# Moving the compressed keys and values of one attention stage ahead of its first scores, on one Trainium2 core

## The reference

```python
kc = einsum('bnlgd,lde->bnge', k_cmp[:, gidx] + cmp_pe[:, None, :], cmp_wk)   # 15 windows of 32 tokens, stride 16
vc = einsum('bnlgd,lde->bnge', v_cmp[:, gidx] + cmp_pe[:, None, :], cmp_wv)
s = q @ kc * scale + bias ; p_cmp = masked_softmax(s) ; o_cmp = p_cmp @ vc      # compressed
o_sel, o_win = ...            # selected blocks and window: with 256 tokens both are dense and causal
o = sum([o_cmp, o_sel, o_win] * sigmoid(h @ w_gate))                           # three gates per head
```

## Time and profile before

| | us |
|---|---|
| three runs | 1266.78, 1266.91, 1272.68 |
| median | 1266.91 |
| the profiled execution's own time | 1268.52 |
| its span in the trace | 1266.7 |
| mean granted TensorE clock | 0.965 |

### The profile page before, as it was taken

The page is one execution under the profiler, slowest core; times in us unless marked ns, Lnnn a source line. Parts: engine busy times, 40 slices in busy tenths (PEclk is TensorE's granted clock), DMA queues, the critical chain, the costliest instruction groups (busy, mean ns, idle before and its releaser), DMA issues.

```text
span 1266.7 us, 19978 instructions
## 1 busy us (share of the span) xinstructions
PE 1159.9 (92%) x8358; PEld 1049.2 (83%) x8358; DVE 933.0 (74%) x1630; ACT 589.4 (47%) x968; POOL 74.4 (6%) x106
## 2 busy tenths in 40 slices
PE   2798798999998977899999989999989988999996
PEld 1687468999897975699999979999979967999996
DVE  5967868888786955598888688887765957765445
ACT  1534655434355455554445464454452365444443
POOL 0000000000000000079000000000000000000000
PEclk8799899999999989999999999999999998999998
DMA  9982335788882960357889637779732452665730
GB/s 375 364 358 74 152 128 196 299 319 286 310 331 100 374 225 1 136 203 277 315 202 368 245 139 296 293 273 292 279 140 101 105 177 85 254 233 200 194 133 34
DMA packets 40810, 280.83 MB, mean 222 GB/s; under 512 B 4736, under 2 KB 5264, under 8 KB 7952
## 3 DMA queue, kind: packets, MB, share of 16 engines
q1 hardware_dynamic: 37296, 269.27, 58.5%
q0 software_dynamic: 2416, 7.92, 2.2%
q10 hardware_dynamic: 1008, 2.37, 0.5%
HBM read 277.91 MB, written 1.10 MB: 220 GB/s over the span
## 4 chain that ended last, share of the span: by engine, by line
PE 69%; DVE 19%; ACT 6%; DMA 5%; issue 1%; SPq 0%; DVEq 0%; ACTq 0%
PE PS L408 68%; DVE LO L1352 5%; DMA raw<-WS 4%; DVE raw L1342 4%; ACT HI L940 2%; DMA SC<-scratch 1%; DVE TMP L1417 1%; DVE SC L1556 1%; DVE TMP L1452 1%; DVE HLo L1412 1%; ACT HH L940 1%; ACT SQ L940 1%; ACT SC L940 1%; DVE SC L1541 1%; DVE RS L1556 1%
## 5 line engine op out<-in xcount | busy, mean ns | idle before, releaser
L408 PE MATMUL PS<-HH,HI 128*128 128x256 f32 x1748 | 502.0, 287 | 25.6 <-ACT HH L940 22.3
L408 PE MATMUL PS<-HLo,HI 128*128 128x256 f32 x1748 | 503.3, 288 | 0.9 <-DVE HLo L1412 0.3
L408 PE MATMUL PS<-HH,LO 128*128 128x256 f32 x1748 | 499.3, 286 | 0.0
L1352 DVE TENSOR_TENSOR LO<-raw,HI 128x1024 fp32r<-128x1024 f32 x340 | 403.8, 1226 | 116.1 <-ACT HI L940 115.9
L940 ACT ACTIVATE HI<-raw 128x1024 fp32r<-128x1024 f32 x340 | 339.8, 1048 | 93.8 <-PE PS L408 64.8
L408 PEld LDWEIGHTS PS<-HH,HI 128*128 128x128 f32 x1748 | 340.0, 195 | 34.9 <-DVE LO L1352 18.9
L408 PEld LDWEIGHTS PS<-HLo,HI 128*128 128x128 f32 x1748 | 339.3, 194 | 4.2 <-DVE HLo L1412 2.9
L408 PEld LDWEIGHTS PS<-HH,LO 128*128 128x128 f32 x1748 | 339.8, 194 | 3.4 <-issue 0.5
L1342 DVE CUSTOM_DVE_ANT_0 raw<-raw,CB,SM 128x1024 f32<-128x1024 f32 x168 | 210.5, 1285 | 24.5 <-DMA raw<-WS 24.5
L408 PE MATMUL PS<-HI,HDH 128*128 128x512 f32 x352 | 140.4, 399 | 0.0
L408 PE MATMUL PS<-HI,HDL 128*128 128x512 f32 x352 | 139.6, 397 | 0.0
(11 more groups left out here) (230 smaller groups left out, 1023.1 us busy)
## 6 DMA issues: line engine op xcount, KB each, us to landing
raw<-WS SPq DMA_DIRECT2D x255, 1024.0 KB, 5.5
SC<-scratch POOLq DMA_DIRECT2D x2, 1024.0 KB, 13.4
FB<-gates_out POOLq DMA_DIRECT2D x3, 512.0 KB, 5.1
SQ<-gates_out POOLq DMA_DIRECT2D x3, 512.0 KB, 9.4
X<-xT ACTq DMA_DIRECT2D x1, 1024.0 KB, 6.9
SC<-ssm POOLq DMA_DIRECT2D x2, 512.0 KB, 5.0
out<-TMP SPq DMA_DIRECT2D x2, 512.0 KB, 2.6
CB<-vecs SPq DMA_DIRECT2D x1, 512.0 KB, 6.5
```

What stands on the lines that cost most here:

```text
L408: return e.matmul(o, l, r, start=start, stop=stop, skip_group_check=True)
L1352: e.tensor_tensor(LO[:, s % HL, :], raw_half(j, h), HI[:, s % HL, :].bitcast(fp32), O.subtract).then_inc(*D.up(("lo", s)))
```

## The change

TensorE: `cmp_keys` and `cmp_values` become `cmp_inputs`, called once ahead of step 0. It does 32 products in turns: key product j into partitions 0 to 63 and value product j into partitions 64 to 127 of one bank, each with 64 columns of weights and 30 moving columns, and signals `cmp_used` with the last. The values so come out turned, with the head's width on the partitions; a new `cmp_spread` in step 0 moves one key head to the upper partitions and transposes the values. The gate products and their two transposes become `gate_values` in step 1, behind the scores of pair 1. ScalarE: three copies out of the bank in `cmp_inputs` ahead of step 0, `cmp_spread` (two copies) after the exponentials of unit 0, the gates' exponential after those of unit 1. VectorE: the windows are formed after ab 3 and ab 4; after ab 7 it says `done` for the chunk at once and calls `low(walk.spare(8))`, ahead of `gate("f0", ...)` and of step 0; the gates' sum and reciprocal stand in step 1 between `biased` of pair 1 and `scaled` of pair 0. The order of the stream, SyncE and GpSimd are as they were.

```diff
--- before.py
+++ after.py
@@ -320,7 +320,7 @@
         gates = GT.rearrange("p (q h c) -> p q h c", q=2, c=3)
         CP = sqf[:, 1152:1392].rearrange("p (q n) -> p q n", q=2)
         ge = sqf[0:24, 1400:1656]
-        kt1 = sqf[0:64, 1656:1671]
+        kt1, vt1 = sqf[0:64, 1656:1671], sqf[64:128, 1656:1686]
         wgh, wgl = [x[:, 0, 0:192].rearrange("p (k n) -> p k n", k=8) for x in (HDH, HDL)]
         gy = [flat(TMP[:, 4 * qt:4 * qt + 4, :]) for qt in range(2)]
         dg = RS[:, 2, :].rearrange("p (q n) -> p q n", q=2)
@@ -666,47 +666,48 @@
                     flip(n // 2 - 1)
             keys_values(("ab", 6))
             values_only(("ab", 7))
-            ps = take("gates")
-            w.wait_ge(*D.at("gatew"))
-            for k in range(8):
-                mm(ps[0:24, 0:256], wgh[:, k, :], HH[:, k, :], k == 0, False)
-                mm(ps[0:24, 0:256], wgl[:, k, :], HH[:, k, :], False, False)
-                i = mm(ps[0:24, 0:256], wgh[:, k, :], HLo[:, k, :], False, k == 7)
-            i.then_inc(*P.up("gates"))
-            banks.give("gates")
-            ps = take("gates2")
-            w.wait_ge(*A.at(("free", "gates")))
-            w.wait_ge(*CONST.at("in"))
-            for qt in range(2):
-                i = e.transpose(ps[:, qt * 24:qt * 24 + 24], ge[:, qt * 128:qt * 128 + 128], C("ident")[0:24, 0:24])
-            i.then_inc(*P.up("gates2"))
-            banks.give("gates2")
-
             cmp_j = where["cmp", 0]
             cmp_w = rawt[:, cmp_j % RAW, :].rearrange("p (s j e) -> p s j e", s=2, j=16)
 
-            def cmp_keys():
+            def gate_values():
+                ps = take("gates")
+                w.wait_ge(*D.at("gatew"))
+                for k in range(8):
+                    mm(ps[0:24, 0:256], wgh[:, k, :], HH[:, k, :], k == 0, False)
+                    mm(ps[0:24, 0:256], wgl[:, k, :], HH[:, k, :], False, False)
+                    i = mm(ps[0:24, 0:256], wgh[:, k, :], HLo[:, k, :], False, k == 7)
+                i.then_inc(*P.up("gates"))
+                banks.give("gates")
+                ps = take("gates2")
+                w.wait_ge(*A.at(("free", "gates")))
+                w.wait_ge(*CONST.at("in"))
+                for qt in range(2):
+                    i = e.transpose(ps[:, qt * 24:qt * 24 + 24], ge[:, qt * 128:qt * 128 + 128], C("ident")[0:24, 0:24])
+                i.then_inc(*P.up("gates2"))
+                banks.give("gates2")
+
+            def cmp_inputs():
+
                 walk.weight(("cmp", 0), 0)
                 ps = take("ck")
                 w.wait_ge(*loaded(cmp_j))
-                w.wait_ge(*D.at(("zc", 0)))
-                for j in range(16):
-                    i = mm(ps[0:64, 0:30], cmp_w[:, 0, j, :], ZC[:, 0, j, :, :], j == 0, j == 15)
-                i.then_inc(*P.up("ck"))
-                banks.give("ck")
-
-            def cmp_values(g):
-                ps = bank("cv") if g else take("cv")
                 w.wait_ge(*D.at(("zc", 1)))
                 for j in range(16):
-                    i = mm(ps[0:15, g * 64:g * 64 + 64], ZC[:, 1, j, g, :], cmp_w[:, 1, j, :], g == 0 and j == 0,
-                           j == 15)
-                if g == 1:
-                    i.then_inc(*P.up("cmp_used"))
-                    walk.done(("cmp", 0), 0)
-                    w.wait_ge(*A.at("kt1"))
-                    mm(ps[64:128, 128:143], C("ident")[0:64, 0:64], kt1, True, True).then_inc(*P.up("cv"))
-                    banks.give("cv")
+                    for t in range(2):
+                        i = mm(ps[64 * t:64 * t + 64, 0:30], cmp_w[:, t, j, :], ZC[:, t, j, :, :], j == 0, j == 15)
+                i.then_inc(*P.up("ck", "cmp_used"))
+                walk.done(("cmp", 0), 0)
+                banks.give("ck")
+
+            def cmp_spread():
+
+                ps = take("cv")
+                w.wait_ge(*A.at("kt1"))
+                mm(ps[64:128, 144:159], C("ident")[0:64, 0:64], kt1, True, True)
+                for g in range(2):
+                    i = e.transpose(ps[0:15, g * 64:g * 64 + 64], vt1[:, g * 15:g * 15 + 15], C("ident")[64:128, 64:128])
+                i.then_inc(*P.up("cv"))
+                banks.give("cv")
 
             def cmp_scores(qt):
                 nk = 7 if qt == 0 else 15
@@ -741,13 +742,13 @@
                            CT[0:nk, 4 * hh + h:4 * hh + h + 2, :], False)
                 x.then_inc(*P.up(("cpv", qt, hh)))
 
-            compressed = {1: [cmp_keys], 2: [lambda: cmp_values(0), lambda: cmp_values(1)],
-                          3: [lambda: cmp_scores(0)], 4: [lambda: cmp_scores(1)],
+            compressed = {0: [cmp_spread], 1: [gate_values], 3: [lambda: cmp_scores(0)], 4: [lambda: cmp_scores(1)],
                           5: [lambda: cmp_turn(0, 0), lambda: cmp_turn(0, 1)],
                           6: [lambda: cmp_turn(1, 0), lambda: cmp_turn(1, 1), lambda: cmp_out(0, 0),
                               lambda: cmp_out(0, 1)],
                           7: [lambda: cmp_out(1, 0), lambda: cmp_out(1, 1)]}
 
+            cmp_inputs()
             for p in range(9):
                 scores("ab", AB, p)
                 if p > 1:
@@ -1124,19 +1125,22 @@
                     flip(n // 2 - 1)
             keys_values(("ab", 6), 0, "kv6")
             values_only(("ab", 7), 128, ("fm", "ab"))
-            w.wait_ge(*P.at("gates"))
-            fn(ge, bank("gates")[0:24, 0:256], F.Exp, scale=-1.0).then_inc(*A.up(("free", "gates")))
-
-            def cmp_keys():
+
+            def gate_values():
+                w.wait_ge(*P.at("gates"))
+                fn(ge, bank("gates")[0:24, 0:256], F.Exp, scale=-1.0).then_inc(*A.up(("free", "gates")))
+
+            def cmp_inputs():
                 high(walk.weight(("cmp", 0), 0))
+                walk.done(("cmp", 0), 0)
                 w.wait_ge(*P.at("ck"))
-                fn(kt1, bank("ck")[0:64, 15:30], F.Copy).then_inc(*A.up("kt1"))
-                fn(KC[0:64, :], bank("ck")[0:64, 0:15], F.Copy).then_inc(*A.up(("free", "ck")))
-
-            def cmp_values():
-                walk.done(("cmp", 0), 0)
+                fn(kt1, bank("ck")[0:64, 15:30], F.Copy).then_inc(*A.up())
+                fn(KC[0:64, :], bank("ck")[0:64, 0:15], F.Copy).then_inc(*A.up())
+                fn(vt1, bank("ck")[64:128, 0:30], F.Copy).then_inc(*A.up(("free", "ck"), "kt1"))
+
+            def cmp_spread():
                 w.wait_ge(*P.at("cv"))
-                fn(KC[64:128, :], bank("cv")[64:128, 128:143], F.Copy).then_inc(*A.up("kc"))
+                fn(KC[64:128, :], bank("cv")[64:128, 144:159], F.Copy).then_inc(*A.up("kc"))
                 fn(VC[0:15, :], bank("cv")[0:15, 0:128], F.Copy).then_inc(*A.up(("free", "cv"), "vc"))
 
             def cmp_exp(qt):
@@ -1151,16 +1155,21 @@
                 fn(flat(CT[0:nk, hh * 4:hh * 4 + 4, :]), bank(("ct", qt, hh))[0:nk, :], F.Copy) \
                     .then_inc(*A.up(("free", ("ct", qt, hh))))
 
-            compressed = {1: [cmp_keys], 2: [cmp_values], 3: [lambda: cmp_exp(0)], 4: [lambda: cmp_exp(1)],
+            compressed = {3: [lambda: cmp_exp(0)], 4: [lambda: cmp_exp(1)],
                           5: [lambda: cmp_turn(0, 0), lambda: cmp_turn(0, 1)],
                           6: [lambda: cmp_turn(1, 0), lambda: cmp_turn(1, 1)]}
 
+            cmp_inputs()
             for p in range(9):
                 for i in (2 * p, 2 * p + 1):
                     if p > 1:
                         moved("ab", i - 4)
                 for i in (2 * p, 2 * p + 1):
                     exps("ab", i, *AB[i])
+                    if i == 0:
+                        cmp_spread()
+                    if i == 1:
+                        gate_values()
                 high(walk.spare(2))
                 for f in compressed.get(p, ()):
                     f()
@@ -1571,9 +1580,6 @@
             w.wait_ge(*A.at("gatew"))
             e.tensor_tensor(HDL[:, 0, 0:192], S("gate"), HDH[:, 0, 0:192].bitcast(fp32), O.subtract) \
                 .then_inc(*D.up("gatew"))
-            for n in range(6):
-                use(("ab", n), 0)
-                use(("ab", n), 1)
             pe2 = S("pe").unsqueeze(2).unsqueeze(3).to_broadcast([128, 16, 2, 15])
 
             def cmp_windows(s):
@@ -1584,16 +1590,22 @@
                     win = bass.AP(src.tensor, src.offset + hp, [list(src.ap[0]), [2, 16], [256, 2], [16, 15]])
                     e.tensor_tensor(ZC[rows, s], win, pe2[rows], O.add).then_inc(*D.up(("zc", s)))
 
-            for n in (6, 7):
+            for n in range(8):
                 use(("ab", n), 0)
                 use(("ab", n), 1)
-                cmp_windows(n - 6)
-            w.wait_ge(*P.at("gates2"))
-            e.tensor_scalar(GT, bank("gates2")[:, 0:48], 1.0, None, O.add).then_inc(*D.up(("free", "gates2")))
-            w.wait_ge(*D.now())
-            e.reciprocal(GT, GT).then_inc(*D.up())
-            w.wait_ge(*D.now())
+                if n in (3, 4):
+                    cmp_windows(n - 3)
```

(18 more changed lines are left out.)

## The result

| | before | changed |
|---|---|---|
| median of 20 runs each, us | 1269.51 | 1273.37 |
| lowest to highest | 1266.24 to 1272.75 | 1268.70 to 1275.72 |
| span of the profiled execution | 1266.7 | 1271.3 |

The ratio is 1.003, with a 95% interval of 1.002 to 1.0041: the changed kernel is 3.9 us slower. Forecast were 4.6 us (1271.5 from a median of 1266.9). The further runs of the kernel before moved its median to 1269.5, so differences are compared, not absolute times.

A forecast was written before the change was run, and what follows sets the result against it. VectorE was taken to lead the attention stage and TensorE to bind from 164.57 us. Pair 0's delay less regained time, +7.7 - 2.1 - 1.0 = +4.6 us, gave a median of 1271.5; range 1266.0 to 1275.5.

The forecast's parts named there:

- the main step: Ahead of pair 0: VectorE waits 10 to 14 us for the load of mod 19; pair 0 starts 7.7 us late.
- What bounds, and that nothing gives time back: Attention stage: VectorE leads, its idle time counts; TensorE bounds from 164.57 us, so time lost before about 164 stays lost.
- Windows earlier, at no cost: Four VectorE additions, 4.09 us, move to about 68 and 74 us, beside TensorE's hold in the flips: gain 0, cost 0.
- Compressed inputs, "full price": Ahead of step 0: 32 products, 64 records at about 0.06 us, take 3.9 us; side by side would be 1.9 less.
- The load, 5.8 us: Load of mod 19 ahead of pair 0, issued at 107.0, takes 5.8 us, bounds 4.7 and 6.89.
- What comes back, 2.1 us by pair 4: Pairs 0 to 4: removed waits and products regain 2.1 us after the slow-clock allowance, bounds 0.8 and 2.8.
- the slack that I let swallow a part of the slow gates: Up to pair 4: of 1.35 us for gate products at half clock, slack takes 0.65.
- Pair 5, 1.0 back: The 1.24 us hole before pair 5 shrinks as TensorE's idle stretch is gone: 1.0 gained, bounds 0 and 1.24.
- Signs: Profile: VectorE idle 10 to 14 us, gates' hole 1.5 to 3, SyncE's wait 12 shorter, gates' clock 0.50, later shift 4 to 5.
- the first, low clock: Stage: load takes 6.9 us, all gate products at 1.2 GHz, pair 5's hole stays: +8.0, 1274.9; chance 0.17.
- the short stall: Pair 0: side-by-side products or 4.7 us load, 4.7 to 5.8 late, 3 to 4 back: +1.5, 1268.4; chance 0.14.
- Paying early is cheaper: Stage: all holes and mod 19's products, 6.97 us, come out in full: -2.3 to -4.3, 1262.6 to 1264.6; chance 0.08.

The follow-up runs named there:

- e8: Changed kernel with all 16 key products first, then all 16 value products, instead of in turns; single run, 1276.26 us.
- e2: Changed kernel with gate_values called ahead of step 0 on all three engines; ratio 1.0019 to the kernel before.
- e3: Kernel before with only gate_values moved to step 1, compressed parts left in steps 1 and 2; ratio 0.999 to the kernel before.
- e4: Changed kernel plus 28 unused products behind cmp_spread in step 0, to keep TensorE busy; ratio 1.0028 to the kernel before.
- e6: Changed kernel without spare(8), products of mod 19 in step 0, gate and its row write behind them; ratio 0.9996 to the kernel before.
- e9: Changed kernel run once more for its profile, nothing altered; single run, 1272.06 us.
- e1: Changed kernel without spare(8), so the products of mod 19 come in step 0 behind biased of pair 0; ratio 1.002 to the kernel before.
- e5: Changed kernel with VectorE's done in step 2, products of mod 19 in step 3, gate directly after ab 7; ratio 0.997 to the kernel before.
- e7: Changed kernel with gate and its row write ahead of spare(8) instead of behind it; single run, 1282.23 us.

## Why the prediction was right, and where it was wrong

The sign was right, and so was the main step: VectorE waits ahead of pair 0 for a load that is only then released (10.51 us, forecast 10 to 14). The closeness of the total, 3.9 us against 4.6, is in part luck. One term was 3 us too dear and one 4 us too generous; they left a stage 6.0 us longer where 4.6 was forecast, and about 2 us came back later, which I had not forecast.

- *What bounds, and that nothing gives time back:* VectorE's holes were the right thing to read. That a shift at 165 us is kept to the end was too simple: the stage lost 6.0 us (6.3 in the repeat), the medians differ by 3.9. The two profiles of the changed kernel show 2.8 and 2.4 us regained later. **What regains it stays open**: over the eleven other profiles the later stages change the difference to before by -3.9 to +3.6 us, without order in the size of the shift.
- *Windows earlier, at no cost:* right. They took 2.03 and 1.94 us at 69.5 and 76.3, and a later LO (86.30) still waited 5.56 us for ScalarE, for 7.74 before.
- *Compressed inputs, "full price":* wrong. I read from the earlier trace rows that a record costs 0.06 us whatever its size, and took that for a limit of issue. It holds for products that follow each other in the same half (e8: 3.5 us); in turns they take 1.8. The Trainium skill's rule on tiling (TensorEngine Tiling (Array Packing), Theoretical Speedup: up to twice), which I set aside, held nearly in full: 3.5 to 1.8.
- *The load, 5.8 us:* the reason was right, its size not. Without a broadcast close ahead it lands in 4.7 to 4.9 (changed, e2, e3, e4, e6, e8, e9), with one 1.1 or 1.2 us ahead in 6.89 and 6.49, behind the row write in 9.7 (e1, e5, e7). With the products' rate this makes pair 0 4.75 us late, not 7.7. That loads grow longer beside another queue's transfers agrees with the Trainium skill (DMA: Bandwidth & Descriptors, Queues, rings and completion order), by which each engine takes turns between queues; the size of the row write's effect does not follow from that.
- *What comes back, 2.1 us by pair 4:* wrong by 4.2; pair 4 came 2.05 us later against pair 0 than before (23.87 for 21.82). The gate products were sized well (14 of 24 slow, 1.5 us more for 1.35), but the scores of pair 1 ran slow too (2.08 us, for 1.14 at full clock in e4), which delayed the gates' start; pair 3 came 1.1 us later than my terms give. Another 0.65 is the slack that I let swallow a part of the slow gates: TensorE's work ahead of pair 4 waits for `biased` of pair 3 (0.70 us idle, released by VectorE), so a delay at pair 3 is handed on. The last 2.4 us are the clock again: from the first `biased` of pair 3 to the end of the scores of pair 4 TensorE took 5.73 us before and 8.13 now. I had counted that stretch at full clock, and e3 and e5 show that it is slow without any stall too.
- *Pair 5, 1.0 back:* 0.8 measured (6.82 us from pair 4 for 7.61), but not for the reason given. "That idle stretch is gone" left out that another slow stretch stands one pair earlier; the 0.8 is less than what that one costs.
- *Signs:* VectorE's idle time, the new hole for the gates (3.04, at the top of 1.5 to 3) and the gates' clock came as said. SyncE's wait shrank by 14.7 us, not 12, and at 172 us the shift was 7.4 (1.4 of it from ahead of the stage), not 4 to 5.
- *Rivals:* the first, low clock, was a part of the truth; the short stall (load of 4.7 us, products side by side) was right for pair 0, but nothing of its 3 to 4 us came back. "Paying early is cheaper" is not borne out by e6: with a wait of 1.12 us the product in step 0 makes the stage 2.5 us longer than in step 3.

So the change is slow because the products of mod 19 are taken before the first scores: their wait holds up pair 0, it leaves TensorE at low clock for the gates behind it, and VectorE has nothing left to do ahead of pair 4, where TensorE is slow in e3 and e5 too. Deleting `low(walk.spare(8))` is not enough, since the products then come in step 0 (e1); with them back in step 3 the rest of the change gains 0.3% (e5), and in the stage all of that gain is had by moving the gates alone (e3).

## What to carry to other kernels

A unit of work that is nearly free where its engine has slack can cost several times its own length when it is moved ahead of the first work of a pipeline (here 9.4 us of the stage for 2.4 us of work): ask when its input is released and who issues that load, and let the walk stop there. When a stall leaves TensorE idle ahead of work on the path, price that work at the low clock. Ask also what an engine will do later, in the place that the work has left. And when an edit moves a small scattered DMA, look at which large load it will stand in front of.

## What the runs showed of the hardware that was not expected

- A 4 KB write in 4-byte pieces takes 9 to 10 us to land and hardly uses the DMA engines by itself (share 0.07 from 108 to 118 us before), and yet a 1 MB load issued 5 us after it takes 9.7 us instead of 4.8, with 41 GB/s moving for 5 us (e1, e5, e7; e6 as the counter-test).
- Plain fp32 products of 128 rows by 64 columns with 30 moving columns take 0.11 us each when one half of the output partitions is filled first and then the other, and 0.06 when they alternate between the halves (e8 and the changed kernel).
- 28 useless products in a stall keep the granted clock at 1.00 through the gate products and shorten the stage by 3.9 us (e4); the time of the whole kernel did not follow (1.0028).
- The same 16 records of TensorE ahead of pair 4 take 2.15 us before and 3.7 to 3.8 in the changed kernel, e3 and e5; the longest idle stretch of TensorE between pair 0 and there is 1.73 us in e5 and 1.60 in e3.
